# The last sigmoid gate of a two-layer decoder trunk, computed with tokens on partitions in place of channels

## What is computed

```python
h = h + squared_relu_mlp(rmsnorm(h, norm_mlp[i]), w_ff1[i], w_ff2[i])
gate = jax.nn.sigmoid(rmsnorm(h, norm_ple[i]) @ w_ple_gate[i])   # 1024 x 1024
h = h + gate * (p[i] @ w_ple_proj[i])                            # 256 x 1024
...
return rmsnorm(h, final_norm)
```

## Time and profile before

| | us |
|---|---|
| median of 3 runs (lowest, highest) | 1614.56 (1613.98, 1615.56) |
| the profiled execution's own time | 1614.48 |
| its span, from the first instruction to the last | 1612.6 |
| PE busy in the span | 1598.4 (99%) |
| DVE, ACT, POOL busy | 906.3 (56%), 607.3 (38%), 65.9 (4%) |
| mean granted TensorE clock | 0.998 of full |

### The profile page before, as it was taken

The page is one execution under the profiler, slowest core; times in us unless marked ns, Lnnn a source line. Parts: engine busy times, 40 slices in busy tenths (PEclk is TensorE's granted clock), DMA queues, the critical chain, the costliest instruction groups (busy, mean ns, idle before and its releaser), DMA issues.

```text
span 1612.6 us, 22051 instructions
## 1 busy us (share of the span) xinstructions
PE 1598.4 (99%) x8244; PEld 1319.4 (82%) x8244; DVE 906.3 (56%) x1585; ACT 607.3 (38%) x1092; POOL 65.9 (4%) x68
## 2 busy tenths in 40 slices
PE   9999999999999999999999999999999999999998
PEld 7888888888888788888888878888878888888887
DVE  5365464464455863635455676777675363535555
ACT  5234334333333531312223445676652222222344
POOL 1000000000000200000001110000020000000111
PEclk9999999999999999999999999999999999999999
DMA  6633433433322333333333333323233333333331
GB/s 165 161 105 96 127 104 93 120 112 86 101 84 69 105 91 103 93 96 94 97 92 103 98 111 92 92 80 93 62 92 103 93 91 104 91 104 91 92 111 72
DMA packets 300571, 160.12 MB, mean 99 GB/s; under 512 B 31545, under 2 KB 295282, under 8 KB 300514
## 3 DMA queue, kind: packets, MB, share of 16 engines
q1 hardware_dynamic: 300112, 158.61, 34.6%
q0 software_dynamic: 144, 0.71, 0.2%
q10 hardware_dynamic: 258, 0.04, 0.0%
HBM read 157.11 MB, written 10.60 MB: 104 GB/s over the span
## 4 chain that ended last, share of the span: by engine, by line
PE 95%; POOL 1%; DVE 1%; DMA 1%; ACT 1%; issue 0%; SPq 0%; POOLq 0%; ACTq 0%; DVEq 0%
PE unit_out L1647 26%; PE unit_out L1649 26%; PE unit_out L1648 25%; PE turned L1723 2%; PE attn L1792 2%; POOL sumsq L862 1%; PE attn L2037 1%; PE unit_out L1811 1%; PE logits L1723 1%; PE unit_out L1812 1%; PE unit_out L1813 1%; DMA w_raw<-in_a_w_qkv_dram 1%; PE logits L1647 1%; PE misc L1723 1%; PE misc L1647 1%; PE misc L1649 1%
## 5 line engine op out<-in xcount | busy, mean ns | idle before, releaser
L1647 PE MATMUL unit_out<-act_hi,w_hi 128*128 128x512 f32 x1849 | 726.5, 393 | 1.4 <-DVE act_lo L1202 1.0
L1649 PE MATMUL unit_out<-act_hi,w_lo 128*128 128x512 f32 x1849 | 718.7, 389 | 0.0
L1648 PE MATMUL unit_out<-act_lo,w_hi 128*128 128x512 f32 x1849 | 718.0, 388 | 0.0
L880 ACT ACTIVATE w_hi<-w_raw 128x1024 fp32r<-128x1024 f32 (+3 forms) x256 | 271.0, 1058 | 459.4 <-PE unit_out L1649 348.2
L1647 PEld LDWEIGHTS unit_out<-act_hi,w_hi 128*128 128x128 f32 x1849 | 347.2, 188 | 76.3 <-DVE w_lo L1187 2.8
L1649 PEld LDWEIGHTS unit_out<-act_hi,w_lo 128*128 128x128 f32 x1849 | 347.1, 188 | 72.5
L1648 PEld LDWEIGHTS unit_out<-act_lo,w_hi 128*128 128x128 f32 x1849 | 347.5, 188 | 69.7 <-issue 0.2
L1187 DVE TENSOR_TENSOR w_lo<-w_raw,w_hi 128x1024 fp32r<-128x1024 f32 (+3 forms) x256 | 320.2, 1251 | 119.3 <-ACT w_hi L880 119.3
L1049 ACT ACTIVATE act_hi<-hidden 128x512 fp32r<-128x512 f32 x64 | 40.5, 633 | 243.4 <-DVE hidden L1445 243.4
L862 POOL TENSOR_TENSOR sumsq<-sumsq,square 128x512 f32<-128x512 f32 x41 | 57.8, 1410 | 1523.9 <-ACT square L908 1522.2
L1442 DVE TENSOR_TENSOR scaled<-unit_out,rstd 128x512 f32<-128x512 f32 x62 | 42.8, 690 | 67.8 <-PE unit_out L1649 67.7
(11 more groups left out here) (291 smaller groups left out, 1414.4 us busy)
## 6 DMA issues: line engine op xcount, KB each, us to landing
w_raw<-in_w_ff_dram SPq DMA_DIRECT2D x128, 512.0 KB, 4.0
w_raw<-in_a_w_qkv_dram SPq DMA_DIRECT2D x56, 512.0 KB, 3.9
w_raw<-in_b_w_qkv_dram SPq DMA_DIRECT2D x24, 512.0 KB, 5.1
w_raw<-in_a_w_qkv_dram SPq DMA_DIRECT2D x32, 256.0 KB, 3.0
w_raw<-in_w_ple_gate_dram SPq DMA_DIRECT2D x16, 512.0 KB, 4.1
bias_tiles_b<-bias_vectors SPq DMA_DIRECT2D x16, 256.0 KB, 4.3
bias<-bias_tiles_b SPq DMA_DIRECT2D x8, 512.0 KB, 3.7
w_raw<-in_a_w_o_dram SPq DMA_DIRECT2D x8, 448.0 KB, 3.6
```

Source lines behind the costliest of these rows:

```text
L880: sc.activation(weights_of(u)[0][:, 0:width, :], w_raw[par][:, 0:width, :], ACT.Copy).then_inc(hi_done, 1)
L1647: te.matmul(bank, w_k[0], hi, start=start, stop=False)
L1648: te.matmul(bank, w_k[0], lo, start=False, stop=False)
L1649: return te.matmul(bank, w_k[1], hi, start=False, stop=stop)
```

## The change

The last gate is turned over: activations' 128x128 blocks (128 channels x 128 tokens) become the stationary operand, and the weights' 128x128 chunk streams past them, so outputs have tokens on partitions. `token_passes` does for each of the four token blocks what `passes` did for all 512 tokens at once. The residual slab `h_b[:, n, :]` is transposed ahead (`turn_h`), and DVE adds it from PSUM and writes straight into `y_out`. The norm's scale becomes one number per partition and block (`start_scale`, 128x4). Sums of squares for the final norm are taken by ACT along the free axis (`accum_out` into `end_squares`), and added up by DVE (`reduce_sum`). The final gain is loaded once, broadcast to all partitions, by an added DMA of SP into `bias[0]`, and POOL multiplies each finished slab of `y_out` by it. In the last half-slabs, the first half's root stands ahead of the second half's sigmoid.

```diff
@@ SP, between the loads of the output projection and of the MLP
             load_out(U_BO, 1, b_w_o[0])
+            sp.wait_ge(logits_done, ITEMS_A + B_HEADS * B_ITEMS)
+            sp.dma_start(end_gain, final_norm.rearrange("(n c) -> n c", n=1)[0:1, :].partition_broadcast(P)
+                         ).then_inc(end_gain_ready, 16)
             load_mlp(U_BF, 1)
@@ POOL
-            for norm in range(1, 7):
-                for n in range(1, KC if norm < 6 else KC - 1):
+            for norm in range(1, 6):
+                for n in range(1, KC):
...
+            pool.wait_ge(end_gain_ready, 16)
+            for n in range(KC - 1):
+                pool.wait_ge(end_squared, n + 1)
+                pool.tensor_tensor(slab_of_y(n), slab_of_y(n), gain_of_slab(n, NT), ALU.mult
+                                   ).then_inc(y_gained, 1)
@@ ACT, gate_of
+                        for a in range(NT):
+                            done = sc.activation(square[n % 2][:, a * P:(a + 1) * P],
+                                                 y_out[:, a, n * P:(n + 1) * P], ACT.Square,
+                                                 accum_out=end_squares[:, a, n:n + 1])
+                        done.then_inc(end_squared, 1)
...
-                        sc.activation(h_a[:, n, :], h_b[:, n, :], ACT.Copy, scale=gains[:, col:col + 1]
-                                      ).then_inc(f_ready, 1)
@@ ACT, the end
             end_sigmoid(0)
+            sc.activation(spare[:, :], eps_col[:, 0:1], ACT.Sqrt)
             end_slab(0)
+            end_stat(0)
             end_sigmoid(1)
             sc.activation(spare[:, :], eps_col[:, 0:1], ACT.Sqrt)
-            end_stat(0)
             end_slab(1)
-            end_row(0)
             end_stat(1)
-            end_row(1)
@@ DVE, gate_of
+                        ve.tensor_tensor(by_token(scaled[:, :]), by_token(unit_out[u.const % 2][:, :]),
+                                         start_scale[:, :].unsqueeze(2).to_broadcast([P, NT, P]), ALU.mult
+                                         ).then_inc(evac_done, 1)
...
-                        ve.tensor_tensor(h_b[:, n, :], hidden[:, :], h_b[:, n, :], ALU.add
+                        ve.wait_ge(h_turned_ps, n + 1)
+                        ve.tensor_tensor(slab_of_y(n), by_token(hidden[:, :]), by_token(end_bank(n)), ALU.add
                                          ).then_inc(gated_ready, 1)
...
-                    if layer == 1 and n > 1:
-                        turned_back(n - 2)
@@ DVE, the end
             end_evac(0)
             end_gated(0)
+            end_sum(0)
             end_evac(1)
-            turned_back(last - 1)
+            end_scales(0)
+            end_row(0, y_ready_even)
             end_gated(1)
-            end_turned(0)
-            end_row(0)
-            end_turned(1)
-            end_row(1)
+            end_row(1, y_ready_odd)
+            end_sum(1)
+            end_scales(1)
+            end_row(2, y_ready_even)
@@ PE
+            def token_passes(bank, blocks, w_k, src, k, start, stop):
+
+                for n, a in enumerate(blocks):
+                    to = bank[:, n * P:(n + 1) * P]
+                    hi, lo = (x[:, k, a * P:(a + 1) * P] for x in src)
+                    te.matmul(to, hi, w_k[0], start=start and n == 0, stop=False)
+                    te.matmul(to, hi, w_k[1], start=False, stop=False)
+                    last = te.matmul(to, lo, w_k[0], start=False, stop=stop and n == len(blocks) - 1)
+                return last
+
+            def token_statistics(norm):
+
+                te.wait_ge(sumsq_done, norm * KC)
+                for a in range(NT):
+                    last = te.matmul(attn[:, a:a + 1], sumsq[:, a * P:(a + 1) * P], ones[:, 0:1],
+                                     start=True, stop=True)
+                last.then_inc(stat_ps, 1)
+
+            def token_gate(first, norm):
+                ple = ple_hi[1], ple_lo[1]
+                for n in range(KC - 1):
...
+                    for k in range(KC):
...
+                        if n == 1 and k == 3:
+                            token_statistics(norm)
+                        token_passes(unit_out[u.const % 2], range(NT), weights(u.const % 2, k), IN[1], k,
+                                     k == 0, k == KC - 1)
...
+                    turn_h(n)
+
+            def turn_h(n):
+
+                wait(te, gated_ready, KC + n - 2)
+                turn(end_bank(n), [(a * P, h_b[:, n, a * P:(a + 1) * P]) for a in range(NT)]
+                     ).then_inc(h_turned_ps, 1)
...
-            gate_of(1, U_BG, 5)
+            token_gate(U_BG, 5)
...
-                    passes(end_unit_bank(hf), weights(u % 2, k), IN[1][0][:, k, cols],
-                           IN[1][1][:, k, cols], k == 0, k == KC - 1)
+                    token_passes(end_unit_bank(hf), blocks, weights(u % 2, k), IN[1], k, k == 0, k == KC - 1)
...
+            turn_h(KC - 1)
             end_unit(0)
             end_unit(1)
-            turn_back(last - 1)
-            end_sum(0)
-            end_turn(0)
-            end_sum(1)
-            end_turn(1)
```

More of the change, by code:

```diff
@@ L912, in statistics @@
                 sc.wait_ge(stat_ps, norm + 1)
-                sc.activation(root[:, :], attn[:, :], ACT.Sqrt, scale=1.0 / D,
+                to, sums = (start_col[:, :], attn[:, 0:NT]) if norm == 5 else (root[:, :], attn[:, :])
+                sc.activation(to, sums, ACT.Sqrt, scale=1.0 / D,
                               bias=eps_col[:, 0:1]).then_inc(root_ready, 1)
@@ L1137, in _ @@
             gate_of(1, U_BG, 5, None)
-            last, w = KC - 1, 7 * KC - 1
-            gain = gains[:, gain_col(w):gain_col(w) + 1]
+            last = KC - 1
             def end_sigmoid(hf):
@@ L1146, in end_slab @@
             def end_slab(hf):
-                cols = slice(hf * HALF, (hf + 1) * HALF)
                 sc.wait_ge(gated_ready, 2 * KC + hf)
[L1149 to L1152, removed]
-            def end_stat(hf):
[L1155 to L1164, removed]
+                sc.wait_ge(end_squared, last)
+                for a in range(hf * NH, (hf + 1) * NH):
+                    done = sc.activation(square[1][:, a * P:(a + 1) * P], hidden[:, a * P:(a + 1) * P],
+                                         ACT.Square, accum_out=end_squares[:, a, last:KC])
+                done.then_inc(end_squared, 1)
+            def end_stat(hf):
+                sc.wait_ge(end_totals, hf + 1)
+                sc.activation(end_col[:, hf * NH:(hf + 1) * NH], end_total[:, hf * NH:(hf + 1) * NH],
+                              ACT.Sqrt, scale=1.0 / D, bias=eps_col[:, 0:1]).then_inc(end_root, 1)
             end_sigmoid(0)
-            sc.wait_ge(sumsq_done, w - 1 - KC)
+            sc.activation(spare[:, :], eps_col[:, 0:1], ACT.Sqrt)
             end_slab(0)
+            end_stat(0)
             end_sigmoid(1)
             sc.activation(spare[:, :], eps_col[:, 0:1], ACT.Sqrt)
-            end_stat(0)
             end_slab(1)
-            end_row(0)
             end_stat(1)
-            end_row(1)
+            a = NT - 1
+            sc.wait_ge(y_gained, last)
+            sc.wait_ge(last_gained, 2)
+            sc.wait_ge(end_rstd, 2)
+            sc.activation(y_out[:, a, :], y_out[:, a, :], ACT.Copy, scale=end_scale[:, a:a + 1]
+                          ).then_inc(y_ready_odd, 1)
         @block.vector
@@ L1622, in end_row @@
-            def end_row(hf):
-                a = hf * NH
-                ve.wait_ge(end_root, hf + 1)
-                ve.reciprocal(end_scale[:, a:a + NH], end_col[:, a:a + NH]).then_inc(end_rstd, 1)
-                ve.wait_ge(f_copied, KC + hf)
-                ve.wait_ge(end_rstd, hf + 1)
+                ve.wait_ge(gated_ready, 2 * KC + hf)
+                ve.wait_ge(end_gain_ready, 16)
+                ve.tensor_tensor(half_of_last_y(hf), by_token(hidden[:, cols]), gain_of_slab(last, NH),
+                                 ALU.mult).then_inc(last_gained, 1)
```

123 lines of the change are left out of this document (65 added, 58 removed).

## The result

| | before | after |
|---|---|---|
| median, us | 1614.65 (1613.98 to 1615.56) | 1748.62 (1736.90 to 1749.98) |
| profiled execution, its span | 1614.48, 1612.6 | 1736.9, 1735.1 |
| mean granted clock | 0.998 | 0.956 (the other three runs: 0.948) |

The ratio is 1.0813, interval 1.0766 to 1.086: 134 us slower, where 52 were forecast and 1678 was the upper end of the range. The sign was right, the size was not.

The account below looks back on a forecast made before the run. PE was taken to bound the last gate, with weight loads setting the new pace: 1614.48 + 53.0 for PE - 0.9 for the tail = 1666.6, stated as 1666.5 us. The 80% range was 1659 to 1678.

Parts of the forecast that it names:

- The price of the 128-column form: Last gate: each 128-column matmul costs 0.112 us, set by its weight load; bounds 0.105 and 0.12.
- The sum for PE: Last gate: 960 matmuls at 0.112 us, turns and sums make 111.5 us against 58.5, so +53.0 us.
- DVE, ACT and POOL hidden: Last gate: their work ends inside each unit of about 13.9 us, so their own changes cost nothing.
- The gain's load at 0: SP's queue: the added 512 KB DMA costs 0, with 1.6 us as the other end.
- The tail: After the last product: 5.2 us from `scaled` to the last row's end, 0.9 us less, bounded by 0 and 1.8.
- rival (e): Last gate: the clock falls to the 1.2 GHz level, 0.224 us per matmul, about 1774 us; chance 3%.
- four matmuls of one column: Norm's sums within the last gate: bound by their loads too, 0.45 us.
- (a): Last gate: loads of the new form take half, 0.067 us per matmul, 1623.5 us; chance 5%.
- (b): Last gate: full rate, a quarter of the columns in a quarter of the time, 0.0567 us, 1613.6 us; chance 3%.
- (c): Last gate: loads partly overlap the preceding matmul's stream, mean start distance 0.081 us, 1637 us; chance 3%.
- (d): Last gate: load and stream in series, 0.165 us per matmul, 1717.6 us; chance 3%.
- A main case of 83%: Whole kernel: loads set the last gate's pace at the full clock, 1666.5 us; chance 83%.

Follow-up runs that it names:

- e1: The changed kernel with the four matmuls for the norm's sums 128 columns wide in place of one, same result: 1667.3 us.
- e2: The kernel before, channels on partitions, with only the last gate's matmuls cut from 512 (256) columns to 128: 1666.85 us.
- f3: The changed kernel with its four one-column matmuls spread, one ahead of each of chunks 0 to 3 of the second unit: 1666.45 us.
- f4: The changed kernel with its one-column group moved whole to behind the first unit's turns: 1667.5 us.
- e4: The changed kernel with four more transposes behind the turns of each unit from the third on: median 1742.47 us, one run of four 1692.2.
- g1: The changed kernel with 32 transposes in a row, once, behind the third unit's turn: median 1691.42 us, one run of four 1671.0 without a fall.
- f1: e2 with four one-column matmuls of unused result ahead of the norm's sums: four runs of 1667.3 to 1669.1 us, two of 1751.6 and 1752.4.
- e3: The changed kernel with one plain fp32 matmul for each triple of fp32r matmuls, the products with the lo parts left out: 1631.35 us.
- f2: The kernel before with four one-column matmuls of unused result ahead of the norm's sums: 1615.37 us, ratio 1.0004.

## Why the prediction was wrong, by its own steps

**The steps that held.** The price of the 128-column form at full rows: 0.112 us, measured 0.112. The sum for PE, 111.5 us: in e1, with the clock up, the stage runs from 1543.4 to 1654.7, 111.4. DVE, ACT and POOL hidden: PE waits for nobody in the stage, and even the old 0.4 us wait is gone. The gain's load at 0: it is 0. The tail 5.2 us: 5.24. One detail in it was different: DVE takes row block 0 between the first half's scale and the second half's product, so the product begins at 1726.54 although the sigmoid is done at 1726.11. The total of these, 1666.5, is what e1 gives, 1667.3 (and e2, f3, f4).

**The step that failed** is the chance of rival (e), "The clock falls", 3%, and the sentence on which it rested: the row of the stage shows 1.00 with PE busy, and "PE would stay as busy by that measure". PE did, and the clock fell all the same. I had noted that the array would stream half of the time, and looked at no more than the average of the stage. What decided was a group that the sum carries as "four matmuls of one column", 0.45 us. It was mis-sized too: each fp32 matmul is two instructions, eight in all, 1561.55 to 1562.41, 0.86 us with next to no columns streaming. The trace of before had shown that, in its tail, where L2072 is recorded `x2` for one matmul (1602.22). In a thin stream that pause tipped the clock in 11 of 12 runs of the kernels that have it unaltered (4 of 4 of the changed kernel, 4 of 4 of e4, 3 of 4 of g1), in two of six in the control f1, and never when spread (f3), widened (e1), put behind the first unit's turns (f4), set among plain fp32 matmuls (e3) or in a dense stream (f2). Behind it the thin stream didn't bring the clock back in 146 us.

**The rival's price** of about 1774 took the fall from the start of the stage, and 0.224 per matmul; the fall came 21 us into it, and a step was 0.213. Where the clock stayed low to the end, the time of the changed kernel was 1748 to 1750. The other rivals are out: (a), (b), (c) and (d) all by the 0.112. (The sum in (d), 0.11 + 0.053, is 0.163; its 0.165 is with 0.112, and 2 us hang on it.)

**The range** should have reached it. A main case of 83% rested on a clock that no row of before showed under such a stream: such fp32r products stand there only in short groups of scores, as at 1012.6, six in 0.4 us with turns and 512 columns behind. That was a resource which the trace didn't show, and it had an upper bound (the half clock) that I priced and then left out.

**What stays open.** Why the same group tips the clock nearly always in one neighbourhood and sometimes in another, and whether turns ahead of it or the burst of loads beside it make the difference; four to six runs per kernel give the frequencies only roughly. Whether the matmuls' data play a part wasn't tried.

## What to carry to other kernels

With fp32r operands of 128 rows and columns, keep 256 columns or more streaming past each weight load: at 512 a matmul costs 0.227 us, at 256 0.12, at 128 0.112, so the last cut nearly doubles the price per column. Where a change leaves PE busy but fewer columns streaming per us, don't take the clock of the stage before for granted: look in the new profile at the granted clock by windows, and find the narrow matmuls that stand ahead of a fall; widening four of them to columns that nobody needs was worth 81 us here. And when a layout is changed for its tail, run its matmul count alone in the old layout first: that one control (e2) priced the whole idea.

## What the runs showed of the hardware that wasn't expected

- The granted clock has a memory. The same stream of 128-column fp32r matmuls ran at 1.00 for the whole stage (e1, e2, f3, f4, over 100 us) and at 0.50 for 146 us (the changed kernel). In these runs it kept whichever level it met. What stood ahead of each fall was 0.86 us of one-column matmuls within it, and of each rise turns in a row (eight in the changed kernel and e4 not dependably, 36 in g1's profile; how densely turns stream no row shows).
- PE's busy share says nothing of this: 20.20 of 20.20 us at 1.00, 146.00 of 146.00 at 0.50.
- At the half clock these matmuls step by 0.213 us, 1.90 times the 0.112 at the full clock and not twice.
